# Scores of two steps in a row in the software-pipelined attention of a two-layer decoder kernel

## Chip, cores, metric

The kernel runs on one core of one Trainium2 chip, as one program. The metric is the device time of one execution in microseconds. The kernel before takes 1911.26 us, the median of 3 runs (1910.68 to 1912.78).

## The reference

Two layers of a hybrid decoder, in float32, for a prompt of 512 tokens and a sample group of 8 sequences of 4 tokens with a paged cache of 1024 tokens. Each layer has an RMS norm, one input projection, retention, block-sparse softmax attention (8 heads of 64), gates, an output projection and a SwiGLU feed-forward part. The change touches only the softmax attention of the prompt. Its queries see their own block of 256 keys causally and the best past blocks, at most three; with 512 tokens there is at most one past block, so every query sees all earlier tokens:

```python
def moba_core(q, kg, vg, valid, k_own, v_own, own_mask):
    qf = q.astype(jnp.float32) * (M_DH ** -0.5)
    s_own = jnp.einsum('hqd,hkd->hqk', qf, k_own.astype(jnp.float32))
    s_own = jnp.where(own_mask[None], s_own, -jnp.inf)
    ...
    s_past = jnp.einsum('hqd,hqnkd->hqnk', qf, kg.astype(jnp.float32))
    s_past = jnp.where(valid[..., None], s_past, -jnp.inf).reshape(H, Q, ks * blk)
    p = jax.nn.softmax(jnp.concatenate([s_past, s_own], axis=-1), axis=-1)
    ...
    return (jnp.einsum('hqnk,hqnkd->hqd', p_past, vg.astype(jnp.float32))
            + jnp.einsum('hqk,hkd->hqd', p_own, v_own.astype(jnp.float32)))
```

## The kernel before

Every engine has its own instruction stream, written out by hand, and runs it in order. Engines wait for each other with semaphores only: a producer counts a semaphore up, a consumer waits until it has reached a number. The 512 prompt tokens and 32 sample tokens are 5 row tiles (4 of 128 rows, one of 32). Large products are made of three matmuls in fp32r (high and low parts); attention runs in plain fp32.

The prompt's attention has 16 steps per layer. Step number s stands for a pair of heads hp = s // 4 and a tile of 128 queries t = s % 4, which looks at the (t+1) * 128 keys up to its own. The two heads of a pair are called z = 0 and 1. The stages of one step, by engine:

- `scores(s)` on TensorE (lines 1029 to 1038): two products of contraction 64, one per head, into PSUM banks 2 + 2 * (s % 2) + z. So steps s and s+2 share their banks, and scores(s) waits on `s_exp` until exp(s-2) has read them. It signals `s_done`.
- `row_max(s)` on VectorE (lines 2203 to 2210): adds the causal mask to the last 128 columns and takes the row minimum of the negated scores; signals `s_max`.
- `exp(s)` on ScalarE (lines 1576 to 1585): two activations from PSUM to the buffer PR (three slots, s % 3), with the row sum read out behind each (ACTIVATION_READ_ACCUMULATOR); signals `s_exp`. It waits until turn_probs(s-3) has read its slot.
- Probabilities on VectorE (lines 2223 to 2229): reciprocal of the sum, two multiplications in PR; signals `s_prob`.
- `turn_probs(s)` on TensorE (lines 1040 to 1052): 2 * (t+1) transposes into banks 6 and 7, once the previous copy has emptied them (`pt_evac`); signals `pt_done`.
- The copy on ScalarE (line 1606): banks 6 and 7 to PT (two slots); signals `pt_evac`.
- `attend(s)` on TensorE (lines 1054 to 1070): 2 * (t+1) products with the values, added up in bank hp % 2. After four steps the bank is copied by ScalarE (`attended`, line 1595) and VectorE (line 2214).

The order of the calls on TensorE is the loop of lines 1072 to 1098. scores(0) and scores(1) stand ahead of it. Step s of the loop then issues scores(s+2), attend(s-3) and turn_probs(s-1). Between them stand pieces of an input projection (`token_part("rqa", ...)`, lines 914 to 916, or line 843 for the sample rows): a whole tile ahead of the loop, three eighths of one at s = 1 and at s = 2 each, a quarter at s = 3, the sample tile at s = 15, and half a tile at s = 16 and behind the loop.

ScalarE's order is the loop of lines 1597 to 1610: exp(0), then in step s exp(s+1), then the copy for step s-1; one rotation's copy (`to_rotate`, line 1524) stands behind step 4's copy, `attended` behind the copy of every step with t = 1 from the second pair on. VectorE's order (lines 2217 to 2233) is row_max(0), row_max(1), then for each s the probabilities of s and row_max(s+2).

Three other queues look at the scores' signal. In the first layer POOL issues the last 34 of 64 copies that lay the cached keys out anew in DRAM (`lay_keys`, lines 719 to 722), number i held until i // 2 scores are done. SP loads keys number 3 once all these copies have landed and all 16 scores are done (lines 588 to 597), and keys 4 and on once TensorE's key score number r-4 is done. Behind the loop TensorE runs `key_scores(0)`, `(1)`, ... (line 1111) for the sample group, mixed with tiles of another projection; each needs its keys loaded and transposed by VectorE (line 2177). In the second layer the keys have been laid out long before.

Of the kernel before, what the change touches and what calls it, by code (L numbers as in the profile page):

```python
# [199 lines left out]
def build(nc, x_prompt, x_sample, cache_k, cache_v, state_ret, page_table, g_mix, w_in, w_br_ret, w_br_att,  # L200
# [586 lines left out]
    def _(pe):  # L787
# [45 lines left out]
        for lay in range(DEPTH):  # L833
# [64 lines left out]
            def token_part(name, f, ks):  # L898

                u, t = row_tile(name, f)  # L900
                n = ROWS[t]
                slot = (U0[name] + u) % 2
                wh = WH[:, slot, :].rearrange("p (k c) -> p k c", c=UC)
                wl = WL[:, slot, :].rearrange("p (k c) -> p k c", c=UC)
                bank, cols = row_bank(name, f)
                out = PS[0:n, bank, cols]
                if ks[0] == 0:
                    split_ready(U0[name] + u)
                    pe.wait_ge(tile_free, lay * NT + T0[name] + f + 1)
                if t == TT - 1:  # L910
                    last = sample_part(slot, bank, (0, 1) if len(ks) == KT else (ks[0] // 4,))
                for k in ks if t < TT - 1 else ():
                    a, b = XH[:, k, t * P:t * P + n], XL[:, k, t * P:t * P + n]
                    pe.matmul(out, a, wh[:, k], start=k == 0, stop=False)  # L914
                    pe.matmul(out, a, wl[:, k], start=False, stop=False)  # L915
                    last = pe.matmul(out, b, wh[:, k], start=False, stop=k == KT - 1)  # L916
                if ks[-1] == KT - 1:
                    last.then_inc(tile_done, 1)
# [110 lines left out]
            def scores(s):  # L1029

                hp, t = divmod(s, 4)
                if s >= 2:
                    pe.wait_ge(s_exp, lay * 16 + s - 1)
                for z in range(2):
                    r = slice(64 * z, 64 * z + 64)
                    last = pe.matmul(PS[:, 2 + 2 * (s % 2) + z, 0:(t + 1) * P], MT[r, hp, t * P:(t + 1) * P],
                                     MT[r, 4 + hp, 0:(t + 1) * P], start=True, stop=True)
                last.then_inc(s_done, 1)

            def turn_probs(s):  # L1040

                t = s % 4
                pe.wait_ge(s_prob, lay * 16 + s + 1)
                if s == 0:
                    pe.wait_ge(rt_taken, 2 * lay + 1)
                if s:
                    pe.wait_ge(pt_evac, lay * 16 + s)
                for z in range(2):
                    for kt in range(t + 1):
                        last = pe.transpose(PS[:, 6 + z, kt * P:(kt + 1) * P],  # L1050
                                            PR[:, s % 3, z, kt * P:(kt + 1) * P], IDENT)
                last.then_inc(pt_done, 1)

            def attend(s):

                hp, t = divmod(s, 4)
                pe.wait_ge(pt_evac, lay * 16 + s + 1)
                if t == 0 and hp >= 2:
                    pe.wait_ge(mo_lo, lay * 4 + hp - 1)
                elif t == 0 and hp == 0:  # L1060
                    pe.wait_ge(own_act, lay * 2 + 1)
                elif t == 0:
                    pe.wait_ge(tile_free, lay * NT + T0["rqa"] + 4)
                for kt in range(t + 1):
                    for z in range(2):
                        last = pe.matmul(PS[64 * z:64 * z + 64, hp % 2, t * P:(t + 1) * P],
                                         MV[:, kt, (2 * hp + z) * 64:(2 * hp + z + 1) * 64],
                                         PT[:, s % 2, z, kt * P:(kt + 1) * P], start=kt == 0, stop=kt == t)
                if t == 3:
                    last.then_inc(pv_done, 1)  # L1070
# [4 lines left out]
            pe.wait_ge(own_act, lay * 2 + 2)  # L1075
            token_part("rqa", 0, kk)
            for s in range(17):
                if s + 2 < 16:
                    scores(s + 2)
                if s == 3:  # L1080
                    token_part("rqa", 1, kk[6:])
                if s == 15:
                    pe.wait_ge(s_exp, lay * 16 + 15)
                    token_part("rqa", 2, kk)
                if s >= 3:
                    attend(s - 3)
                if s == 1:
                    pe.wait_ge(tile_free, lay * NT + T0["rqa"] + 3)
                    token_part("rqa", 1, kk[:3])
                if s == 2:  # L1090
                    token_part("rqa", 1, kk[3:6])
                if s == 16:
                    token_part("rqa", 3, kk[:4])
                if s:
                    turn_probs(s - 1)
# [913 lines left out]
    def _(dve):  # L2009
# [65 lines left out]
        for lay in range(DEPTH):  # L2075
# [665 lines left out]
            def part_added(s):  # L2741

                _, c, i = STEPS[s]
                if c == 0:
                    dve.wait_ge(xf_back[i], lay * 16 + 16)
                copies_made(s)
                odd = halves(XP[:, 2 * i + 1, :])
                dve.tensor_tensor(odd, odd, halves(EB[:, 1, :]), ALU.add).then_inc(val_ready, 1)
                done(T0["sv"] + 2 * s + 1)
                even = halves(XP[:, 2 * i, :])  # L2750
                dve.tensor_tensor(even, even, pair[2 * (s % 2)], ALU.add)
                dve.wait_ge(val_ready, lay * NVAL + V0N["gu"] + NC + s + 1)
                dve.tensor_tensor(odd, odd, pair[2 * (s % 2) + 1], ALU.subtract).then_inc(tile_free, 2)
# [146 lines left out]
```

## Time and profile before

| | |
|---|---|
| time, median of 3 runs | 1911.26 us (1910.68 to 1912.78) |
| time of the profiled execution | 1911.65 us |
| its span, first to last instruction | 1910.0 us |
| busy: TensorE, VectorE, ScalarE, POOL | 1890.1, 1332.2, 811.5, 201.6 us |
| mean granted TensorE clock | 0.999 |
| attention loop of the first layer, first scores in it to the first key score | 103.62 to 145.48 us |
| the same in the second layer | 1046.44 to 1088.28 us |

Engines are named PE (TensorE matmul), PEld (its weight loads), DVE (VectorE), ACT (ScalarE), POOL and SP. Matmuls are pipelined, and the ends of their records are modelled, so a record reaches a little into the next one. "L1036" is a line of the kernel; L1036 is the scores, L1050 the transposes, L1066 the attend products, L1583 the exp, L1606 the copy, L1111 the key scores. Neighbouring records of the same kind are merged into one row with their number (x4). A bracket gives the idle time of the engine ahead of the row and what released it. A fp32 product shows as two records, so scores of one step are x4, and scores of two steps in a row are x8, named by the first one's shape.

### The profile page before, as it was taken

To read this page: it belongs to the slowest core of one execution; us is meant where nothing else is said; L and a number is where in the kernel's file an instruction comes from. 1 tells how busy PE (TensorE), PEld (TensorE's weight loads), DVE (VectorE), ACT (ScalarE), POOL (GpSimd) and SP (SyncE) were. 2 spreads that over 40 slices of the span, in tenths; PEclk is the share of its full clock that TensorE was granted. 3 is DMA by queue.
4 is the path that set the end of the run, shared out by engine and by line. 5 is a ranking of instruction groups with operands and counts; after the bars stand their busy time and mean duration, and the time that the engine had idled before them with its cause. 6 is when DMAs were issued, how large, how long until landed. Compare 5 with 4: busy or idle time off the path is not lost. (4 is left out here: it accounts for less than half of the span.)

```text
span 1910.0 us, 38191 instructions
## 1 busy us (share of the span) xinstructions
PE 1890.1 (99%) x15595; PEld 1745.4 (91%) x15595; DVE 1332.2 (70%) x1903; ACT 811.5 (42%) x1277; POOL 201.6 (11%) x289
## 2 busy tenths in 40 slices
PE   9999999999999999999999999999999999999999
PEld 7768879989999999999977797899899999999999
DVE  5787544367765898988667774444686568889876
ACT  4372323234434464655434633233244344555454
POOL 1350110012000011212000002101110000000000
PEclk9999999999999999999999999999999999999999
DMA  7868871355244346666444388423543442433332
GB/s 257 298 196 301 286 255 56 99 167 169 89 158 136 89 146 178 169 179 170 135 161 158 100 290 296 156 78 111 182 153 112 125 130 83 135 106 93 105 101 86
DMA packets 268958, 300.51 MB, mean 157 GB/s; under 512 B 14538, under 2 KB 213362, under 8 KB 268274
## 3 DMA queue, kind: packets, MB, share of 16 engines
q1 hardware_dynamic: 243634, 208.53, 34.6%
q0 software_dynamic: 25024, 89.41, 14.4%
q8 instruction: 123, 2.02, 0.4%
q14 instruction: 49, 0.40, 0.1%
q10 hardware_dynamic: 128, 0.15, 0.0%
HBM read 273.00 MB, written 58.59 MB: 174 GB/s over the span
## 5 line engine op out<-in xcount | busy, mean ns | idle before, releaser
L2081 DVE TENSOR_TENSOR WL<-RAW,WH 128x2048 fp32r<-128x2048 f32 (+2 forms) x76 | 161.1, 2120 | 75.0 <-ACT WH L1502 74.9
L934 PE MATMUL PS<-XH,WH 128*128 128x272 f32 x960 | 203.3, 293 | 0.6
L934 PE MATMUL PS<-XL,WH 128*128 128x272 f32 x960 | 198.3, 288 | 0.0
L934 PE MATMUL PS<-XH,WL 128*128 128x272 f32 x960 | 197.8, 287 | 0.0
L1502 ACT ACTIVATE WH<-RAW 128x2048 fp32r<-128x2048 f32 (+2 forms) x84 | 149.9, 1785 | 45.7 <-PE PS L934 18.5
L1408 PE MATMUL PS<-KQ,CH 128*128 128x272 f32 x1088 | 158.3, 288 | 1.5 <-DVE KQ L2687 1.5
L934 PEld LDWEIGHTS PS<-XH,WH 128*128 128x128 f32 x960 | 150.4, 188 | 7.8 <-issue 5.2
L934 PEld LDWEIGHTS PS<-XL,WH 128*128 128x128 f32 x960 | 150.9, 188 | 0.0
L914 PE MATMUL PS<-WH,XH 128*128 128x256 f32 x512 | 150.6, 294 | 0.1
L934 PEld LDWEIGHTS PS<-XH,WL 128*128 128x128 f32 x960 | 150.3, 189 | 0.0
L1408 PEld LDWEIGHTS PS<-KQ,CH 128*128 128x128 f32 x1088 | 145.0, 188 | 2.3 <-issue 2.3
L915 PE MATMUL PS<-WL,XH 128*128 128x256 f32 x512 | 145.0, 283 | 0.0
L916 PE MATMUL PS<-WH,XL 128*128 128x256 f32 x512 | 143.9, 281 | 0.0
L698 POOL DMA_DIRECT2D keys_laid<-in_cache_k x128 | 95.7, 747 | 230.7 <-issue 215.8
L914 PEld LDWEIGHTS PS<-WH,XH 128*128 128x128 f32 x512 | 96.6, 189 | 24.0 <-issue 21.8
L916 PEld LDWEIGHTS PS<-WH,XL 128*128 128x128 f32 x512 | 97.3, 190 | 0.0
L915 PEld LDWEIGHTS PS<-WL,XH 128*128 128x128 f32 x512 | 96.6, 189 | 0.0
L1913 ACT ACTIVATE EB<-PS 128x272 f32<-128x272 f32 x96 | 38.1, 397 | 129.6 <-PE PS L1408 127.5
L2699 DVE TENSOR_TENSOR CH<-RAW,CH 128x1536 fp32r<-128x1536 f32 x44 | 77.2, 1756 | 12.6 <-ACT CH L1895 12.6
L1709 ACT ACTIVATE EB<-EA 128x544 f32<-128x544 f32 x36 | 23.6, 656 | 133.5 <-DVE EA L2376 87.0
L2722 DVE TENSOR_TENSOR CH<-RAW,T34H 128x1024 fp32r<-128x1024 f32 x46 | 56.2, 1221 | 22.3 <-ACT T34H L1909 22.3
L2108 DVE SCALAR_TENSOR_TENSOR EA<-EA,CL 128x128 f32<-128x128 f32 x80 | 23.3, 291 | 66.6 <-ACT EA L1524 48.0
(465 smaller groups left out, 5093.0 us busy)
## 6 DMA issues: line engine op xcount, KB each, us to landing
RAW<-in_w_in SPq DMA_DIRECT2D x94, 512.0 KB, 5.8
keys_laid<-in_cache_k POOLq DMA_DIRECT2D x128, 256.0 KB, 3.7
RAW<-in_w_gu SPq DMA_DIRECT2D x128, 256.0 KB, 4.3
PG<-keys_laid SPq DMA_DIRECT2D x16, 1024.0 KB, 8.1
RAW<-in_w_down SPq DMA_DIRECT2D x64, 256.0 KB, 4.4
RAW<-in_w_gu SPq DMA_DIRECT2D x24, 512.0 KB, 5.1
PG<-in_cache_v POOLq DMA_DIRECT2D x40, 256.0 KB, 4.5
PG<-in_cache_v SPq DMA_DIRECT2D x40, 256.0 KB, 4.4
```

What stands on the lines that cost most here:

```text
L698: pool.dma_start(KEYS.ap()[lay, r, b].rearrange("(g k) (c d) -> (k c) g d", g=4, c=4), src.rearrange("p (g d) -> p g d", g=4)).then_inc(ke ...
L914: pe.matmul(out, a, wh[:, k], start=k == 0, stop=False)
L915: pe.matmul(out, a, wl[:, k], start=False, stop=False)
L916: last = pe.matmul(out, b, wh[:, k], start=False, stop=k == KT - 1)
L934: last = pe.matmul(PS[:, 2 * pair + h, 0:HALF], w[:, i, c0:c0 + P], block[:, h * HALF:(h + 1) * HALF], start=first and i == 0 and a == 0, ...
L1408: last = pe.matmul(PS[:, bank, 0:HALF], a[:, k, :], moving(n - 1, k, low), start=start and k == m == 0, stop=k == HK - 1 and m == 2, skip_ ...
L1502: act.activation(WH[:, slot, 0:n], RAW[:, slot, 0:n], ACT.Copy).then_inc(hi_ready, 1)
L1709: act.activation(EB[:, dst, :], EA[:, src, :], ACT.Sigmoid).then_inc(sig_done, 1)
L1913: act.activation(dst, PS[:, src, 0:HALF], ACT.Copy).then_inc(copied, 1)
L2081: dve.tensor_tensor(WL[:, slot, 0:n], RAW[:, slot, 0:n], WH[:, slot, 0:n].bitcast(F32), ALU.subtract).then_inc(lo_ready, 1)
L2699: dve.tensor_tensor(a_part(s, 1), raw_chunks(s % 2)[:, 1:4], a_part(s, 0).bitcast(F32), ALU.subtract).then_inc(la_ready, 1)
L2722: dve.tensor_tensor(t34(s, 1), raw_t34(s % 2), t34(s, 0).bitcast(F32), ALU.subtract).then_inc(lo_ready, 1)
```

## The change

At every even step of the loop, TensorE now issues scores(s+2) and scores(s+3) one behind the other, and none at odd steps. Nothing else is changed: no instruction, wait, buffer or semaphore is added or taken away.

```diff
             for s in range(17):
-                if s + 2 < 16:
+                if s % 2 == 0 and s + 2 < 16:
                     scores(s + 2)
+                    scores(s + 3)
                 if s == 3:
                     token_part("rqa", 1, kk[6:])
                 if s == 15:
```

## Rows read from the trace of the kernel before

**Rows 1.** Busy time per engine in the loop of the second layer, granted clock, DMA.

```profile
core 0: us, PE busy (x) PEld busy (x) DVE busy (x) ACT busy (x) POOL busy (x), PEclk, DMA share, GB/s
...
1046.44:1088.28 41.84, 40.59 (x361) 27.56 (x361) 31.36 (x80) 28.48 (x79) 0.00 (x0) 1.00 0.16 51
```

**Rows 2.** TensorE timeline, first layer: start, duration, engine, line, operation.

```profile
103.62 1.77 PE L1036 MATMUL PS<-MT 64*128 64x384 f32 x8
```

**Rows 3.** TensorE timeline, second layer, steps 2 and 3; idle before in brackets.

```profile
1050.57 0.39 PE L914 MATMUL PS<-WH,XH 128*128 128x256 f32 x1
...
1051.74 0.60 PE L1050 MATMUL PS<-FIX,PR 128*128 128x128 f32 x4
1052.69 0.70 PE L1036 MATMUL PS<-MT 64*128 64x256 f32 x4 [0.35 <-ACT PR L1583]
```

**Rows 4.** TensorE timeline, second layer, steps 6 to 13 and what follows.

```profile
1060.96 1.09 PE L1066 MATMUL PS<-PT,MV 128*64 128x128 f32 x16
1061.98 0.66 PE L1050 MATMUL PS<-FIX,PR 128*128 128x128 f32 x4
1062.57 0.70 PE L1036 MATMUL PS<-MT 64*128 64x256 f32 x4
...
1065.36 0.66 PE L1066 MATMUL PS<-PT,MV 128*64 128x128 f32 x8
1065.95 1.09 PE L1050 MATMUL PS<-FIX,PR 128*128 128x128 f32 x8
1066.97 1.13 PE L1036 MATMUL PS<-MT 64*128 64x512 f32 x4
...
1075.71 1.13 PE L1036 MATMUL PS<-MT 64*128 64x512 f32 x4
...
1088.28 1.96 PE L1111 MATMUL PS<-PG,QB 128*32 128x128 f32 x64
```

**Rows 5.** ScalarE timeline of the same steps.

```profile
1055.51 0.81 ACT L1606 ACTIVATE PT<-PS 128x768 f32<-128x768 f32 x1 [1.69 <-PE PS L1050]
...
1058.89 0.47 ACT L1524 ACTIVATE EA<-PS,SM 128x256 f32<-128x256 f32 x1
...
1060.76 0.69 ACT L1583 ACTIVATE PR<-PS,SM 128x512 f32<-128x512 f32 x1
...
1062.68 0.60 ACT L1606 ACTIVATE PT<-PS 128x512 f32<-128x512 f32 x1 [0.47 <-PE PS L1050]
1063.17 0.59 ACT L1595 ACTIVATE MOH<-PS 128x512 fp32r<-128x512 f32 x1
1063.65 0.37 ACT L1583 ACTIVATE PR<-PS,SM 128x128 f32<-128x128 f32 x1
...
1065.19 0.47 ACT L1583 ACTIVATE PR<-PS,SM 128x256 f32<-128x256 f32 x1
...
1066.00 0.21 ACT L1583 ACTIVATION_READ_ACCUMULATOR PR<-PS,SM 128x1 f32 x1
1067.08 1.03 ACT L1606 ACTIVATE PT<-PS 128x1024 f32<-128x1024 f32 x1 [0.87 <-PE PS L1050]
1068.00 0.57 ACT L1583 ACTIVATE PR<-PS,SM 128x384 f32<-128x384 f32 x1
```

**Rows 6.** Timelines of POOL and then TensorE, first layer, around the loop's end.

```profile
143.62 0.74 POOL L698 DMA_DIRECT2D keys_laid<-in_cache_k  x1 [0.42 <-issue]
...
145.48 1.95 PE L1111 MATMUL PS<-PG,QB 128*32 128x128 f32 x64
...
155.30 1.71 PE L1111 MATMUL PS<-PGK,QB 128*32 128x128 f32 x32 [2.96 <-DVE PGK L2177]
...
161.88 1.08 PE L1111 MATMUL PS<-PG,QB 128*32 128x128 f32 x32 [0.81 <-DVE PG L2177]
```

**Rows 7.** TensorE timeline, second layer, key score 4.

```profile
1099.93 1.08 PE L1111 MATMUL PS<-PG,QB 128*32 128x128 f32 x32 [0.87 <-DVE PG L2177]
```

**Rows 8.** Busy time and granted clock behind the wait of the first layer.

```profile
157.00:159.00 2.00, 1.88 (x10) 1.90 (x10) 1.97 (x7) 0.35 (x1) 0.00 (x0) 0.50 1.04 387
```

## Prediction

> **What bounds the kernel now.** I first read the busy time of each engine over the prompt's attention of the second layer (1046.44 to 1088.28 us) [rows 1]. TensorE works 40.59 of 41.84 us, VectorE 31.36, ScalarE 28.48. So TensorE sets the pace, but a step passes through all three engines: scores(s) on TensorE, mask and minimum on VectorE, exp(s) on ScalarE, probabilities on VectorE, turn_probs(s) on TensorE, the copy of what was turned on ScalarE (copy(s) below), attend(s) on TensorE. TensorE stays busy only because its next instruction is always one whose inputs were made a step earlier. Where it is short of such work it waits for an exp already: 0.35 us ahead of scores(5) [rows 3].
>
> Second view: TensorE's timeline [rows 2 to 4], for the price of each call. Records overlap by about 0.07 us, so I take start to next start, or the record less 0.07. With t = s % 4: scores cost 0.63 (t=1, 0.70 less 0.07) and 1.06 (t=3); attend 0.59 (t=1), 0.81 (t=2: half way between 0.59 and 1.02), 1.02 (t=3); turn_probs 0.59 (t=1) and 1.02 (t=3).
>
> Third: ScalarE's timeline [rows 5], whose records overlap by some 0.10. Copies: 0.49 (t=1), 0.71 (t=2), 0.92 (t=3), so some 0.30 for t=0. exp(t=1) runs from 1065.19 to 1066.00 + 0.21: 1.02 us until its signal, 0.90 until the next instruction starts. The other widths differ by twice the difference of one activation: 0.70 until the next start for t=0, 1.10 for t=2, and 1.46 until the signal for t=3. From the start of turn_probs to the start of its copy pass 0.70 us (1061.98 to 1062.68, t=1) and 1.13 (1065.95 to 1067.08, t=3). From an exp's end to the scores that wait for it I take 0.05.
>
> **The change, part by part.** Number and size of instructions are unchanged on every engine, and so are all waits. What moves is scores(s+3), for s = 2, 4, ..., 12, from the head of step s+1 to the head of step s. (At s = 0 nothing changes: step 0 holds nothing behind scores(2), so scores(3) follows it already.) The moved call brings its wait along: scores(s+3) needs exp(s+1), which gives its banks back. Queued behind that wait on TensorE are now attend(s-3), turn_probs(s-1) and, at s = 2, three eighths of a projection tile.
>
> When is exp(s+1) ready? ScalarE's order is exp(s), copy(s-2), exp(s+1), copy(s-1). So exp(s+1) stands behind copy(s-2), which needs turn_probs(s-2), the last thing TensorE did before step s. Before, attend(s-3) and turn_probs(s-1) ran on TensorE meanwhile: that was the cover. Now only scores(s+2) does, 0.4 to 0.85 us. The chain becomes serial from pair to pair, from the start of one odd scores to the start of the next:
>
> scores(5) to scores(7). scores(5) starts where it did, since exp(3) is untouched. Before, copy(2) began 2.82 us later (1052.69 to 1055.51) [rows 3, 5]. The token piece (1050.57 to 1051.74, 1.17) and turn_probs(1) (0.59), which stood ahead of scores(5), now stand behind it: 4.58. Then copy(2) 0.71, exp(5) 1.02, 0.05: 6.36.
> scores(7) to (9). scores(7) 1.06, attend(1) 0.59, turn_probs(3) until its copy 1.13, copy(3) 0.92, a rotation's copy 0.36 (line 1524) [rows 5], exp(6) 1.10, copy(4) 0.30, exp(7) 1.46, 0.05: 6.97.
> scores(9) to (11). 0.63, attend(3) 1.02, turn_probs(5) until its copy 0.70, copy(5) 0.49, the high part of an attended pair 0.48 (line 1595), exp(8) 0.70, copy(6) 0.71, exp(9) 1.02, 0.05: 5.80.
> scores(11) to (13). As (7) to (9) without the rotation: 6.61. scores(13) to (15): 5.80.
>
> Together 31.54 us from scores(5) to scores(15), against 23.02 now (1052.69 to 1075.71) [rows 3, 4]: 8.5 more. Then the tail: attend(9) 0.59 and turn_probs(11) 1.02 now stand behind scores(15), not ahead of it, 1.6 more; and turn_probs(12) waits for copy(11), since no scores stand between the two turns: 1.13 + 1.03 + 0.05 after the start of turn_probs(11), against 1.02 + 0.81 of TensorE's own work, 0.4. Behind that all is as it was. **10.5 us per layer**.
>
> What is saved? Two scores calls in a row cost less than two apart: scores(2) and (3) take 1.77 less 0.07 [rows 2], against 1.06 and an estimated 0.84 apart, so 0.2 us per pair, 2.4 us for twelve. But it shortens scores(s+2), and behind that TensorE now waits for exp(s+1); the wait grows by the same 0.2. I cost it at nothing.
> The Trainium skill, TensorEngine Tiling (Array Packing), Key Properties, says that a change of tiling mode drains TensorE, which speaks for fewer changes; going by that alone the change would be a gain. The row agrees that adjacency saves, but it is worth only the 0.2 us above.
>
> VectorE gets scores(s+3) a step early and has more room. POOL's queue takes the scores' signal: its last two key copies of the first layer wait for scores(15). The last is issued at 143.62 [rows 6]; scores(15) would be done about 142.6 (132.9 + 8.5 + 1.2), but scores(14) and (13) before it are late too. I bound the delay of that queue by 0 and 4 us. SP issues the load of keys 3 behind scores(15) and POOL's last copy; no other DMA hangs on these signals.
>
> **What of it reaches the end.** Second layer: TensorE's next wait is 0.87 us for turned keys [rows 7], and these keys are loaded after TensorE's own first key score, so the wait moves along. All 10.5 count. First layer: ahead of key score 3 TensorE waits 2.96 us for keys that come from POOL's chain, not from TensorE, and 0.81 us ahead of key score 4 [rows 6]. If TensorE comes 10.5 us later, at 162.8 instead of 152.3, the keys (155.3, plus at most 4) are there. The stretch from key score 0 to key score 4 takes 16.40 us in the first layer (145.48 to 161.88) and 11.65 in the second (1088.28 to 1099.93) [rows 4, 6, 7]. I take the second layer's value for the changed first: 4.75 us come back, part of it because the clock, granted at 0.50 from 157 to 159 behind that wait [rows 8], would stay up. 10.5 - 4.75 = 5.8.
>
> Sum: 10.5 + 5.8 = 16.3. The profiled execution took 1911.65 us, 0.4 above the median: 1911.26 + 16.3 = **1927.5**.
>
> **The rivals.**
> (A) Less than the sum, chance 0.12. The chain is shorter than I walk it (ScalarE picks up sooner, a copy overlaps), or the first layer hides all of its share. With only the second layer paying: 1922; with two thirds of that loss, 1918. Against it: the walk names a dependency for each step.
> (B) The clock falls, 0.10. TensorE waits 2.1 us ahead of scores(5) (from 1050.57, where scores(4) gives way, to 1052.69) [rows 3] and some 1 us ahead of each later pair. For: behind a 2.96 us wait the granted clock fell to 0.50 [rows 6, 8]. Against: that is the only such place here, and it was longer. There key score 3 took 1.71 us against 1.08 for key score 4 [rows 6], 0.6 more, and the 2 us at 0.50 behind it [rows 8] lose 1.0. With 1.6 us for a drop and three drops in each layer, 9.6 more: 1937.
> The Trainium skill, TensorE: Matmul & The Clock Gate, A second HAM failure mode: psum-queue depth-cycling, describes a kernel whose short, frequent idle between groups of matmuls made the clock swing between its levels; by it this case would be likelier. The trace speaks against it so far: with waits of 0.35 us the loop holds 1.00 [rows 1].
> (C) The other side: no loss, 0.05. The pair saves its 0.2 us twelve times and the 0.35 us wait shrinks, some 3 us: 1908. It decides at exp(s+1): were it done before scores(s+2) ends, 0.4 to 0.85 us after turn_probs(s-2), nothing would wait. Against: the copy and the exp alone need some 1.75 us after that turn (0.30 + 1.46, or 0.71 + 1.02).
> (D) The order does not matter, 0.03: TensorE waits here but the first layer's key wait and later ones take it up. That needs slack in the second layer, and no row shows more than 0.87 us: 1911.
>
> **How the numbers follow.** My forecast, both layers' loops longer and the first layer giving 4.75 us back, has 0.70. Its own spread: with nothing given back 1932, and 1 us either way in each layer's walk: 1923 to 1933. (A) carries the low end to 1918, (B) the high end to 1937. A measurement of this kernel can tell 0.2%, 3.8 us. Slower by more: forecast, A, B: 0.92. Within: D and half of C: 0.05. Faster: the rest of C, 0.03.
>
> **What the changed profile would show.** TensorE's waits on ScalarE's exp (line 1583 as releaser, at the scores) grow to some 10 us per layer, the largest 2.1 us ahead of scores(5); scores with even number run alone, with a wait between the two of a pair. From the first key score to the fifth the first layer takes about 11.7 us, without the 2.96 us wait, at a clock of 1.00. scores(5) to scores(15) takes about 31.5 us. ScalarE waits for turn_probs as before, VectorE has more idle. Wrong I am if the pairs run as one block, if exp(s+1) ends before scores(s+2), if the granted clock in the loop is under 1.00, or if later waits for keys shrink or grow in the second layer.

## Result and profile after

The changed kernel takes 1935.87 us (median of 4, 1933.95 to 1937.95), the kernel before beside it 1911.61: a ratio of 1.0127, 95% interval 1.0114 to 1.0140, 24.3 us slower. The sum of the prediction had 16.3 us, its range reached to 1937 us. The profiled execution is the longest of the four, 1937.95 us, with a span of 1936.3.

First view, the stretches of the changed kernel: length, busy time (with instructions) of TensorE, weight loads, VectorE, ScalarE and POOL, then granted clock, DMA share, GB/s. The first row is the first layer's loop; then three pieces of it, the stretch from key score 0 to key score 4, the second layer's loop, and again key score 0 to 4.

```profile
103.06:160.60 57.54, 46.54 (x361) 31.81 (x360) 33.31 (x80) 27.78 (x77) 23.95 (x32) 0.88 0.57 168
110.00:113.40 3.40, 3.40 (x18) 3.40 (x17) 1.49 (x4) 0.25 (x1) 2.24 (x3) 0.51 0.73 221
123.70:127.10 3.40, 3.18 (x21) 2.20 (x22) 2.54 (x6) 0.17 (x2) 2.05 (x3) 0.52 0.36 94
137.30:144.10 6.80, 6.24 (x34) 4.23 (x34) 3.72 (x10) 2.14 (x8) 3.13 (x4) 0.50 0.61 175
160.60:172.27 11.67, 10.79 (x195) 9.71 (x193) 11.17 (x24) 3.22 (x7) 0.00 (x0) 1.00 1.05 374
1056.83:1114.56 57.73, 46.65 (x362) 31.83 (x361) 32.13 (x80) 27.78 (x79) 0.00 (x0) 0.88 0.12 37
1114.56:1126.21 11.65, 10.78 (x194) 9.71 (x193) 11.16 (x24) 3.21 (x7) 0.00 (x0) 1.00 0.80 287
```

The reader is to see three things. Both loops are some 15.8 us longer than before (41.84 in [rows 1]). TensorE does the same instructions, yet its busy time went from 40.59 to 46.65 us, and its clock from 1.00 to 0.88: in three pieces of the first loop (rows 2 to 4) it ran at 0.5. The second loop has three such pieces as well (1062.2 to 1069.0, 1079.4 to 1082.6, 1093.0 to 1096.4 us); in each loop two last 3.4 us and one lasts 6.8. And the first layer's stretch from key score 0 to 4 is now 11.67 us, where it was 16.40 [rows 4, 6]; it is like the second layer's.

Sum for this execution: 15.7 + 15.9 - 4.7 = 26.9, against 26.3 between the two spans; the first loop starts 0.6 us earlier here (103.06 against 103.62).

Each edit moves the lines behind it down by a few: in the changed kernel L1584 is the exp, L1607 the copy and L1112 the key scores. Second view, TensorE's waits in the first and, behind the dots, in the second layer of the changed kernel (total, number, longest):

```profile
PE PS L1036 <- ACT PR L1584: 9.2, 10, 2.1
PE PS L1050 <- ACT PT L1607: 1.8, 5, 0.4
...
PE PS L1036 <- ACT PR L1584: 9.2, 11, 2.0
PE PS L1050 <- ACT PT L1607: 1.9, 5, 0.4
PE PS L1112 <- DVE PG L2178: 0.9, 1, 0.9
```

The 2.96 us wait for keys in the first layer [rows 6] is gone. The waits for exp grew to 9.2 us per layer, and turn_probs waits for the copy of the previous turn five times.

Third view, TensorE's timeline of the changed kernel, second layer, from scores(10) to scores(13), at full clock until 1092.6:

```profile
1084.40 0.92 PE L1036 MATMUL PS<-MT 64*128 64x384 f32 x4 [0.25 <-ACT PR L1584]
1086.01 1.13 PE L1036 MATMUL PS<-MT 64*128 64x512 f32 x4 [0.70 <-ACT PR L1584]
1087.07 0.66 PE L1066 MATMUL PS<-PT,MV 128*64 128x128 f32 x8
1087.66 1.09 PE L1050 MATMUL PS<-FIX,PR 128*128 128x128 f32 x8
1088.68 0.88 PE L1066 MATMUL PS<-PT,MV 128*64 128x128 f32 x12
1089.96 0.41 PE L1050 MATMUL PS<-FIX,PR 128*128 128x128 f32 x2 [0.40 <-ACT PT L1607]
1090.99 0.49 PE L1036 MATMUL PS<-MT 64*128 64x128 f32 x4 [0.62 <-ACT PR L1584]
1092.60 0.91 PE L1036 MATMUL PS<-MT 64*128 64x256 f32 x4 [1.12 <-ACT PR L1584]
```

scores(11) to scores(13) takes 6.59 us (1086.01 to 1092.60); the walk had 6.61. There is a wait between the two scores of each pair, so nowhere in this chain do they run as one block.

Fourth view, the first layer of the changed kernel: POOL issues its last key copy, and VectorE turns the keys for key score 3.

```profile
152.40 0.74 POOL L698 DMA_DIRECT2D keys_laid<-in_cache_k  x1 [0.41 <-issue]
...
163.32 2.30 DVE L2178 STREAM_TRANSPOSE PGK<-PGK 128x2048 f32<-128x2048 f32 x1
```

The last copy is issued 8.8 us later than before (143.62 [rows 6]), more than the 4 us that the prediction allowed. The keys are turned at 165.62, and TensorE comes to key score 3 at 167.28: they are there with 1.7 us to spare.

### The profile page after: what moved, and what is told of

Read it like the earlier page. It is cut to its first block and busy times, and to the rows that moved or that the text cites. A ratio compares the mean times of both kernels' runs of the same rounds, so it can differ in the third digit from the quotient of the medians.

```text
span 1936.3 us, 38191 instructions
## 1 busy us (share of the span) xinstructions
PE 1899.9 (98%) x15595; PEld 1752.3 (90%) x15595; DVE 1334.4 (69%) x1903; ACT 809.8 (42%) x1277; POOL 201.6 (10%) x289
## 5 line engine op out<-in xcount | busy, mean ns | idle before, releaser
L2719 DVE TENSOR_TENSOR CH<-RAW,CH 128x1024 fp32r<-128x1024 f32 x46 | 56.3, 1224 | 19.3 <-ACT CH L1903 19.2
```

The costliest lines, as they stand in the source:

```text
L2719: dve.tensor_tensor(t12(s, 1), raw_t12(s % 2), t12(s, 0).bitcast(F32), ALU.subtract).then_inc(l12_ready, 1)
```

## Experiments

Two theories for the 8 us between sum and result. **Clock**: the walk is right, and the waits let the clock fall, each fall costing some 1.6 us. **Walk too short**: dependencies cost more than walked, and the clock only shows it. Beside them the walk itself is tested: that it counts what is queued behind the wait for exp(s+1), and that copy(s-2) stands ahead of that exp. Where a kernel below has additional transposes of the identity, they write where the next products overwrite.

### The waits filled (e1_fill)

```diff
                 if s % 2 == 0 and s + 2 < 16:
                     scores(s + 2)
+                    for i in range({2: 13, 4: 5, 6: 6, 8: 3, 10: 6, 12: 3}.get(s, 0)):
+                        pe.transpose(PS[:, max(s - 3, 0) // 4 % 2, ...], IDENT, IDENT)
                     scores(s + 3)
```

> The changed kernel with identity transposes (0.13 us each; 13, 5, 6, 3, 6, 3 of them in steps 2, 4, 6, 8, 10, 12) between scores(s+2) and scores(s+3), where TensorE would wait; they end before the wait does and write where attend(s-3) writes next. Theory 1 (the walked waits give 10.5 us per loop, the low clock the other 5.3): the granted clock stays at 1.00 in both loops, each loop takes about 52.4 us instead of 57.6, time about 1926 to 1928 us. Theory 2 (the walk itself was too short, the clock is a bystander): loops stay at 57 us or more, time 1935 or more. If idle sequences of TensorE other than this wait (ahead of scores(s+2), ahead of turn_probs) are enough to lower the clock, it falls in spite of the filling and the time lies between.

Measured: 1927.92 us (1927.08 to 1928.98), ratio 1.0087 (1.0070 to 1.0103). The same windows of this kernel, the two loops:

```profile
103.31:155.44 52.13, 45.74 (x397) 31.38 (x397) 32.95 (x80) 27.67 (x77) 24.08 (x32) 1.00 0.63 186
1051.63:1103.73 52.10, 45.74 (x397) 31.36 (x396) 32.02 (x80) 27.78 (x79) 0.00 (x0) 1.00 0.13 41
```

The clock stays at 1.00 and the loops take 52.1 us. TensorE has more instructions than in the changed kernel, its chain is the same, and the kernel is 8.0 us faster: the clock is the cause of that part. What remains is 16.1 us over the kernel before, where the sum had 16.3. From scores(5) to scores(15) this kernel takes 31.23 us in both layers; the walk had 31.54, and the changed kernel takes 36.66 and 36.86. "Walk too short" falls. How a fill looks, first layer, around scores(8) and (9) (line 1081 is the fill):

```profile
121.03 0.49 PE L1036 MATMUL PS<-MT 64*128 64x128 f32 x4 [0.99 <-ACT PR L1586]
121.46 0.87 PE L1081 MATMUL PS<-FIX 128*128 128x128 f32 x6
122.64 0.70 PE L1036 MATMUL PS<-MT 64*128 64x256 f32 x4 [0.32 <-ACT PR L1586]
```

The wait in front of scores(9) is 0.32 instead of 1.12 us. The 0.99 in front of scores(8) is not filled; with the shorter waits that are left it did not lower the clock.

### One pair alone, and all but that one (e2_pair_step2, e3_pairs_from4)

e2:

```diff
-                if s % 2 == 0 and s + 2 < 16:
+                if s + 2 < 16 and s - 1 not in (2,):
                     scores(s + 2)
+                if s in (2,):
                     scores(s + 3)
```

e3 has (4, 6, 8, 10, 12) in place of (2,).

> Only the pair of step 2 (scores(4), scores(5)) stands together, all others as before. Walk: the wait ahead of scores(5) grows to 2.1 us, the loop gets 1.8 us longer, 43.7 instead of 41.9; in the first layer the wait for keys takes it up, so the time is 1911.6 + 1.8 = 1913.4 us. If one wait of 2.1 us is enough to lower the clock, each loop loses up to 1.6 us more (1915); if it takes many waits in a row, the clock stays at 1.00.

> Pairs at steps 4 to 12 only, scores(5) as before. Walk: 8.7 us per loop (50.6), less 4.75 in the first layer: 1911.6 + 12.6 = 1924 us with the clock up. If many waits of about 1 us lower the clock without the long one, some 4 us more per layer: 1932; if the clock needs the long wait of step 2, it stays up and 1924 holds.

Measured: e2 1915.65 us (1912.97 to 1917.28, 10 runs), where 1913.4 was expected, ratio 1.0020 (1.0010 to 1.0030); e3 1928.98 us (1927.91 to 1931.23), ratio 1.0094 (1.0077 to 1.0111). The loops of e2, then of e3:

```profile
102.63:148.78 46.15, 43.19 (x362) 29.75 (x361) 32.22 (x80) 28.49 (x77) 23.81 (x32) 0.93 0.64 189
1048.97:1092.31 43.34, 40.40 (x362) 27.52 (x361) 31.45 (x80) 28.59 (x79) 0.00 (x0) 1.00 0.15 50
```

```profile
103.37:155.43 52.06, 42.54 (x362) 28.54 (x361) 32.76 (x80) 27.57 (x77) 24.04 (x32) 0.97 0.61 185
1051.66:1104.55 52.89, 43.62 (x362) 29.35 (x361) 32.05 (x80) 27.78 (x79) 0.00 (x0) 0.94 0.12 41
```

TensorE's timeline: scores(5) of e2 in the first and in the second layer, then e2's key score 4 in the first layer; last, scores(13) of e3 in the first layer.

```profile
108.92 1.22 PE L1036 MATMUL PS<-MT 64*128 64x256 f32 x4 [2.08 <-ACT PR L1585]
...
1055.22 0.70 PE L1036 MATMUL PS<-MT 64*128 64x256 f32 x4 [2.04 <-ACT PR L1585]
...
162.89 1.91 PE L1113 MATMUL PS<-PG,QB 128*32 128x128 f32 x32 [2.12 <-DVE PG L2179]
...
133.57 1.23 PE L1036 MATMUL PS<-MT 64*128 64x256 f32 x4 [1.12 <-ACT PR L1585]
```

In e2 the second layer kept its clock and its loop is 1.5 us longer (walked: 1.8). In the first layer, with the same wait of 2.1 us, the clock fell for 6.8 us, and the loop is 2.8 us longer than the second's. One wait of 2.1 us thus is enough in some cases and not in others. The clock accounts for a part of the 4.3 us between e2's fastest and slowest run: the mean clock over the whole program is 0.999 in the fastest and 0.997 in the four slowest.

The expectation that the wait for keys takes up what the first layer loses did not hold. That loop is 4.3 us longer (46.15 against 41.86), and the stretch from key score 0 to key score 4 gave back 2.3 (14.11 against 16.40). TensorE no longer waits 2.96 us ahead of key score 3 but 0.21, and instead 2.12 ahead of key score 4, whose keys are turned at 162.83; the clock fell once more there, and key score 4 took 1.91 us instead of 1.08.

In e3, where no wait in the loop is over 1.12 us, the clock fell once in each loop (0.97 and 0.94). So neither expectation on what it takes holds alone: a long wait can do it, many short ones can too. The price of a fall: e3's walk gives 41.9 + 8.7 = 50.6, the loops took 1.5 (a fall of 3.4 us) and 2.3 more (one of 6.8 us).

### ScalarE's order (e4_exp_first)

```diff
             for s in range(17):
-                if s + 1 < 16:
+                if s + 1 < 16 and (s % 2 or s in (0, 14)):
                     exp(s + 1)
+                if s % 2 and s < 12:
+                    exp(s + 2)
```

> The changed kernel, but ScalarE runs exp(s+1) ahead of copy(s-2) for the second scores of each pair (exp 3 to 13). Theory: copy(s-2) stands in the chain ahead of exp(s+1), so the wait ahead of scores(s+3) shrinks by that copy (0.7 us for pairs at 4, 8; 0.3 at 6, 10), and the loop by some 2.7 us: 7.7 instead of 10.5 per layer at full clock, time 1922 with the clock up and about 1930 with it falling as in the changed kernel. Rival (exp(s+1) is late because of VectorE's minimum, not because of ScalarE's queue): the waits stay and the time stays at 1936 or grows, since the copy is later for turn_probs.

Measured: 1928.45 us (1927.64 to 1929.71), ratio 1.0086 (1.0069 to 1.0103); loops of 52.48 and 53.86 us at a clock of 0.93 and 0.90, with two falls of 3.4 us in the first and three in the second. ScalarE's timeline, then TensorE's, both of this kernel, second layer, around scores(7):

```profile
1065.16 0.47 ACT L1584 ACTIVATE PR<-PS,SM 128x256 f32<-128x256 f32 x1
1065.52 0.20 ACT L1584 ACTIVATION_READ_ACCUMULATOR PR<-PS,SM 128x1 f32 x1
1065.61 0.81 ACT L1609 ACTIVATE PT<-PS 128x768 f32<-128x768 f32 x1
```

```profile
1064.53 0.92 PE L1036 MATMUL PS<-MT 64*128 64x384 f32 x4
1065.77 1.13 PE L1036 MATMUL PS<-MT 64*128 64x512 f32 x4 [0.33 <-ACT PR L1584]
```

exp(5) is done at 1065.72, 0.05 ahead of scores(7), and copy(2) follows it. The wait is 0.33 us; it was 0.96. So the copy did stand in the chain, and the rival, VectorE's minimum, is not what made exp(5) late. The time is 7.4 us below the changed kernel's; with fewer waits the clock also fell less, so the size of the order alone comes from the next run.

### Both at once (e8_fill_exp_first)

e4's edit, with e1's fill at 13, 4 and 4 transposes in steps 2, 6 and 10.

> Both at once: ScalarE's exp(s+1) ahead of copy(s-2), and TensorE's waits filled (13, 4, 4 transposes at steps 2, 6, 10). Theory: the two losses are independent and add up: loops of about 49.4 us at a clock of 1.00, time 1911.8 + 7.5 + 2.8 = 1922 us. If the remaining waits still lower the clock, 1.5 us more for each drop (two in each layer: 1928, as without the filling).

Measured: 1923.75 us (1922.88 to 1924.42), ratio 1.0065 (1.0049 to 1.0080).

```profile
103.66:153.25 49.59, 43.65 (x382) 29.78 (x382) 32.95 (x80) 27.74 (x77) 24.15 (x32) 1.00 0.62 185
1050.30:1099.85 49.55, 43.63 (x383) 29.75 (x382) 31.97 (x80) 27.84 (x79) 0.00 (x0) 1.00 0.14 43
```

49.6 us per loop at full clock, against 52.1 with ScalarE's old order: the order is worth 2.5 us per loop (walked: 2.7). The loops were expected at 49.4 us; the time is 1.8 us over the expected 1922, of which the loops have some 0.3 and the stretch to key score 4 another 0.3 (11.98 us, not 11.65); the rest is not accounted for. Against these loops those of e4 are 2.9 us (two falls) and 4.3 us (three falls) longer: 1.4 us for each fall of 3.4 us.

### The second scores behind attend (e7_behind_attend)

```diff
                 if s % 2 == 0 and s + 2 < 16:
                     scores(s + 2)
-                    scores(s + 3)
 ...
                 if s >= 3:
                     attend(s - 3)
+                if s % 2 == 0 and s + 2 < 16:
+                    scores(s + 3)
```

> The changed kernel with scores(s+3) behind attend(s-3) instead of ahead of it, still ahead of turn_probs(s-1). Theory: what counts is what stands behind the wait for exp(s+1). attend(s-3) is cover again (0.6 or 1.0 us) for the pairs from step 4 on, so the waits ahead of the second scores fall from 0.96, 1.12, 0.70 to about 0.4, 0.2, 0.2; ahead of scores(5) 2.1 stays. The loop is 6.6 us longer than before instead of 10.5 at full clock: 1911.8 + 6.6 + 1.9 = 1920 us, 1.5 more for each drop of the clock, so up to 1924. Rival (the two scores must be adjacent to gain anything, and the loss comes from the clock): it would be slower than the changed kernel, since the mode changes are back.

Measured: 1922.83 us (1921.15 to 1926.33), ratio 1.0062 (1.0046 to 1.0077). Its loops:

```profile
103.43:153.28 49.85, 42.43 (x361) 29.06 (x361) 32.85 (x80) 27.67 (x77) 24.22 (x32) 0.97 0.62 182
1049.80:1099.63 49.83, 42.45 (x362) 28.77 (x361) 32.12 (x80) 27.78 (x79) 0.00 (x0) 0.97 0.13 43
```

TensorE's timeline, second layer, scores(7), then scores(9):

```profile
1063.69 1.13 PE L1036 MATMUL PS<-MT 64*128 64x512 f32 x4 [0.38 <-ACT PR L1585]
...
1070.05 0.70 PE L1036 MATMUL PS<-MT 64*128 64x256 f32 x4
```

The wait ahead of scores(7) is 0.38 us as expected, and those ahead of scores(9), (11), (13) and (15) are gone. The kernel is 13 us faster than the changed one by moving one call past another; a part of it is the clock. 49.8 is 1.4 over the walk's 48.4, and the clock fell once in each loop, for 3.4 us. What is queued behind the wait thus counts; the rival, that adjacency carries the gain, does not hold.

### What adjacency is worth (e9_split_pair)

```diff
+                if s == 1:
+                    pe.transpose(PS[:, 0, 0:P], IDENT, IDENT)
                 if s + 2 < 16:
                     scores(s + 2)
```

> The kernel before, with one identity transpose (128 rows of contraction) between scores(2) and scores(3), which stand in a row there without any wait between them (scores(2) to the next call: 1.70 us in both layers). If adjacency is worth 0.2 us per pair because nothing of another shape stands between, the stretch takes 1.70 + 0.13 + 0.2 = 2.0 us or somewhat more; if the shape in between does not matter, 1.83. The time of the kernel changes by less than can be measured.

Measured: 1911.33 us, a single run. TensorE's timeline, first layer:

```profile
103.00 0.92 PE L1036 MATMUL PS<-MT 64*128 64x384 f32 x4
103.84 0.33 PE L1079 MATMUL PS<-FIX 128*128 128x128 f32 x1
104.11 1.13 PE L1036 MATMUL PS<-MT 64*128 64x512 f32 x4
105.16 0.39 PE L914 MATMUL PS<-WH,XH 128*128 128x256 f32 x1
```

103.00 to 105.16 is 2.16 us, 0.46 more than the 1.70 of the unbroken pair [rows 2]. 0.13 is the transpose's own time (13 in a row took 1.64 us in e1), and some 0.3 goes with the change of shape, there and back. The scores alone now take 0.84 and 1.05, as elsewhere in the loop. The Trainium skill, TensorEngine Tiling (Array Packing), Key Properties, says that a change of tiling mode drains TensorE. The trace agrees with a price for such a change, here 0.3 us for a round trip, but does not tell it from a price of going from a product to a transpose. And none of it came out in the loop, which is as long as before (41.82 us), since TensorE's next wait for exp (0.45 us, at scores(4)) is gone.

### The price of a clock drop where TensorE waits for keys (e5_before_fill)

```diff
                 for f in value_rows(q):
                     token_part("rv", f, kk)
+                if lay == 0 and q == 3:
+                    for i in range(18):
+                        pe.transpose(PS[:, 2, 256:384], IDENT, IDENT)
                 key_scores(q)
```

> The kernel before, with 18 identity transposes (2.3 us) in the first layer's 2.96 us wait for keys ahead of key score 3. Theory: they keep the clock at 1.00, where it fell to 0.50 for 3.4 us behind that wait; the 1.5 us that such a drop cost in the loops of the last four kernels are won, and key score 3 takes 1.08 us instead of 1.71: 1910.3 us. Rival: what TensorE wins there it waits longer for the next keys (0.81 us ahead of key score 4 grows), so the time stays at 1911.8 within 0.3.

Measured: 1911.62 us (11 runs), the kernel before beside it 1911.70, ratio 1.0000 (0.9991 to 1.0009). TensorE's timeline of this kernel:

```profile
152.06 2.19 PE L1167 MATMUL PS<-FIX 128*128 128x128 f32 x18
155.18 1.08 PE L1111 MATMUL PS<-PGK,QB 128*32 128x128 f32 x32 [0.94 <-DVE PGK L2180]
161.77 1.08 PE L1111 MATMUL PS<-PG,QB 128*32 128x128 f32 x32 [1.66 <-DVE PG L2180]
```

The clock stayed up and key score 3 took 1.08 us, but the wait ahead of key score 4 is 1.66 instead of 0.81 [rows 6], and key score 0 to 4 takes 16.50 us (16.40 before). The rival of this run is right: at this place the drop cost nothing, since the next keys set the pace.

## Why the prediction held, and where it fell short

**Sign and range**: right; 1935.87 lies inside 1918 to 1937, near its upper end. The likeliest case was 1927.5, and the result came out as rival (B), to which I gave 0.10: it lies in the range by that rival alone, as the forecast's own spread ended at 1933.

**The walk** of 31.54 us from scores(5) to scores(15), the tail, and 10.5 us per layer: right. Where the clock stays up (e1) that stretch takes 31.23 us and the loops are 10.3 us longer than before. In the changed kernel the waits ahead of the second scores and at turn_probs (2.1, 0.96, 1.12, 0.70, and 0.40) are the ones that the walk implies; those ahead of the first scores of a pair (0.98, 0.62, 0.25) it left unnamed, but the exps that end them are links of the same chain. e8 has a link changed at full clock and came within 0.3 us per loop. So did e7, if 1.4 us is taken off for its one fall; that price is from e4 and e8.

**What reaches the end**: right. The first layer gave back 4.73 us (16.40 to 11.67), the second nothing. But a part of the reason was wrong: I counted on the clock in that stretch as a part of the gain. e5 shows that the clock there was free; the 4.7 us are the wait for keys that TensorE no longer reaches too early.

**POOL and SP**: the outcome right, the bound wrong. Key score 3 does not wait in the changed kernel, as forecast. But POOL's last copy came 8.8 us later, not 0 to 4. With the loop of the sum it would have been 4.0 (147.60 in e1), at the edge of the bound. The keys were in time by 1.7 us all the same, since late scores hold back the copies and TensorE alike: the forecast did not fail there, but not for the reason given. And e2 shows that this wait does not take up a smaller loss whole.

**The saving by adjacency**: "I cost it at nothing" holds. The waits stand between the two scores, and in e9 breaking the one pair that runs unbroken did not lengthen the loop.

**The step that failed** is the reading of the clock in (B): "Against: that is the only such place here, and it was longer." I took the absence of falls at waits of 0.35 us as evidence for waits of 1 to 2 us, where the kernel before had none to show. The clock fell three times in each loop, as (B) had it, and with waits no longer than 1.12 us too (e3). The granted clock of 0.88 in the loops is also one of the signs that I had named for being wrong, and scores(5) to scores(15) took 36.7 and 36.9 us instead of 31.5. (B)'s size was 9.6 us; measured were 8.0 between the medians of the changed kernel and e1, and 11.0 between the loops of the two profiled executions (57.54 + 57.73 - 52.13 - 52.10). The case should have had the larger chance. The Trainium skill, TensorE: Matmul & The Clock Gate, A second HAM failure mode: psum-queue depth-cycling, tells of a kernel in which frequent short idle between groups of matmuls made the clock swing between its two levels; the changed kernel's trace agrees (0.88 over both loops), and I had set it aside for want of a row.

Open is what decides whether it falls in a given loop: e2 had the same wait of 2.1 us in both layers and a fall in one. Not tried was a pairing with a fourth buffer of probabilities, so whether that would keep TensorE supplied is not shown.

## To carry to other kernels

Calls with the same wait semaphores are not equal in cost wherever they stand: in a pipeline over several engines that is walked in order, ask of a moved call not what it costs but what is queued behind its wait, and whether the other engine can even have started what it waits for. Where a change gives a busy TensorE waits that it did not have, price the clock as well: some 1.5 us for a fall of 3.4 us here, 2.3 to 2.8 for one of 6.8, together a third of the loss. A few transposes of the identity inside a wait are a quick test for it: they separate the wait from the clock, as e1 did. And where a wait on a second chain is to take up a loss, look at the next wait of that chain too: in e2 the keys of the following score took its place.

## What the runs showed of the hardware

- The granted clock fell to 0.50 with waits of at most 1.12 us in the loop (e3), and stayed at 1.00 with waits of up to 0.99 us when the others were filled (e1), and behind a long one of 2.04 us (e2, second layer), where one of 2.08 us in the first layer had it fall.
- At the low level (0.50) a projection product took 0.21 us from one matmul to the next against 0.12. A fall of 3.4 us cost 1.4 to 1.5 us of the loop (e4 against e8, e3), one of 6.8 us 2.3 (e3) and 2.8 (e2).
- Two fp32 products of contraction 64 with one 128-row transpose between them took 0.46 us more than without it, 0.3 beyond the transpose's own 0.13 (e9).
- More instructions, less time: e1 adds 36 transposes per layer and is 8.0 us faster than the kernel without them.
